# Two combines taken apart tile by tile, and a down projection moved ahead of the last expert tile

## What is computed

```python
def rmsnorm(x, g):
    y = xf * lax.rsqrt(jnp.mean(xf * xf, axis=-1, keepdims=True) + EPS)
    return (y * g).astype(x.dtype)

for l in range(DEPTH):
    u = modulate(rmsnorm(h, norm_mix[l]), m_lat[0], m_lat[1])
    ...
    h = h + m_lat[2] * y
    v = modulate(rmsnorm(h, norm_ffn[l]), m_lat[3], m_lat[4])
    f = hier_moe(v)
    h = h + m_lat[5] * f
return rmsnorm(h, norm_final)
```

## Time and profile before

| | |
|---|---|
| median of three runs | 2790.07 us (2789.45 to 2794.46) |
| the profiled execution's own time | 2781.04 us |
| its span, first to last instruction | 2779.2 us |
| PE busy | 2543.3 us, 92% of the span |
| DVE, ACT, POOL busy | 1035.4, 330.2, 238.7 us |
| combine to first projection, layer 0 | 1586.4 to 1632.4 us |
| first addition of the last combine to the end of the span | 2741.25 to 2779.2 us |

### The profile page before, as it was taken

How to read it: one execution, slowest core, us unless ns; L and a number is a source line. 1 busy time by engine, 2 the same in 40 slices (tenths; PEclk the granted TensorE clock), 3 DMA queues, 4 the chain that set the end, 5 groups by cost and what they waited for, 6 DMA issues and landing times. The chain is left out here.

```text
span 2779.2 us, 32467 instructions
## 1 busy us (share of the span) xinstructions
PE 2543.3 (92%) x14177; PEld 1115.0 (40%) x14178; DVE 1035.4 (37%) x1986; ACT 330.2 (12%) x640; POOL 238.7 (9%) x225
## 2 busy tenths in 40 slices
PE   6999999989999979999999769999997999999991
PEld 2556455544445533333333334444454333333330
DVE  2855246774845632222222241101364222222214
ACT  3100123331101100000000030000011000000001
POOL 2000000002830000000000000000000000000000
PEclk8888988998999979999999779999996999999996
DMA  9663000021030179999999531101004899999975
GB/s 331 211 241 136 16 23 23 23 99 61 0 113 39 65 296 388 390 378 398 386 376 386 202 107 46 46 23 61 16 31 187 332 386 373 385 396 390 368 307 230
DMA packets 121866, 574.11 MB, mean 207 GB/s; under 512 B 11743, under 2 KB 48807, under 8 KB 94712
## 3 DMA queue, kind: packets, MB, share of 16 engines
q1 hardware_dynamic: 103016, 523.32, 49.3%
q0 software_dynamic: 18704, 48.66, 4.5%
HBM read 550.71 MB, written 38.01 MB: 212 GB/s over the span
## 5 line engine op out<-in xcount | busy, mean ns | idle before, releaser
L1536 PE MATMUL ps<-arena 128*32 128x512 f32 x6144 | 695.6, 606 | 43.5 <-DMA arena<-in_ex_w_dram 43.5
L1536 PEld LDWEIGHTS ps<-arena 128*32 128x32 f32 x6144 | 199.8, 111 | 471.2 <-issue 471.2
L1560 PE MATMUL ps<-arena 128*32 128x512 f32 x3072 | 342.9, 598 | 22.7 <-DMA arena<-in_ex_w_dram 22.6
L1636 PE MATMUL ps<-arena 128*128 128x512 f32 x768 | 331.7, 595 | 1.8 <-ACT arena L833 1.8
L2156 DVE TENSOR_SCALAR arena<-ps,gain_x,mod 128x128 f32<-128x128 f32 x384 | 126.8, 403 | 380.0 <-PE ps L1521 380.0
L1413 PE MATMUL ps<-arena 128*128 128x512 f32 x512 | 228.5, 601 | 7.6 <-DVE arena L2264 6.1
L1636 PEld LDWEIGHTS ps<-arena 128*128 128x128 f32 x768 | 146.6, 191 | 186.5 <-issue 186.5
L1560 PEld LDWEIGHTS ps<-arena 128*32 128x32 f32 x3072 | 107.9, 111 | 248.7 <-issue 248.6
L2188 DVE SCALAR_TENSOR_TENSOR arena<-ps,arena,gates 128x512 f32<-128x512 f32 x96 | 72.1, 751 | 267.8 <-PE ps L1560 267.8
L1230 PE MATMUL ps<-arena 128*128 128x512 f32 x384 | 167.3, 593 | 0.7 <-ACT arena L863 0.7
L2164 DVE TENSOR_TENSOR arena<-arena,ps 128x512 f32<-128x512 f32 x48 | 52.6, 1096 | 275.0 <-PE ps L1536 275.0
(11 more groups left out here) (266 smaller groups left out, 2159.9 us busy)
## 6 DMA issues: line engine op xcount, KB each, us to landing
arena<-in_ex_w_dram SPq DMA_DIRECT2D x192, 2048.0 KB, 13.1
arena<-in_mod_w_dram SPq DMA_DIRECT2D x24, 2048.0 KB, 9.5
arena<-expert_rows SPq DMA_DIRECT2D x16, 1024.0 KB, 8.1
arena<-in_od_w_in_dram SPq DMA_DIRECT2D x24, 512.0 KB, 6.6
normed_rows<-arena POOLq DMA_DIRECT2D x16, 512.0 KB, 2.9
arena<-in_ev_w_in_dram SPq DMA_DIRECT2D x3, 2048.0 KB, 13.7
arena<-in_ev_w_in_dram SPq DMA_DIRECT2D x12, 512.0 KB, 4.1
arena<-in_x_dram POOLq DMA_DIRECT2D x1, 4096.0 KB, 22.0
```

The costliest lines, as they stand in the source:

```text
L1536: ins = nc.tensor.matmul(bank(2 + m)[c:c + n], x[:, j, c:c + n], w_slot(e % 2, m, KC, FE)[:, j], start=j == 0, stop=j == KC - 1)
L1560: ins = nc.tensor.matmul(bank(5 + half)[c:c + n], HT[:, j * P + c:j * P + c + n], w_slot(e % 2, 2, FC, D)[:, j, half * 512:(half + 1) * 51 ...
L1636: ins = nc.tensor.matmul(bank(2 * k + half), w[:, k, j], u_part(half, j), start=j == 0, stop=j == KC - 1)
```

## The change

It has four parts.

1. *Last pass.* On PE the down projection of pass 22 stands ahead of the up projections of pass 23 instead of behind them; on DVE the scaling of pass 22 stands ahead of the hidden product of pass 23. SP's loads are not changed.
2. *Pair sums.* For tiles 1, 3, 5 and 7 of each combine POOL adds the two expert rows (`pair_sums`), and DVE adds that sum to `H`: one addition of DVE instead of two, and one more of POOL.
3. *Norm by tile.* After layer 0 each tile goes through square, root, norm, transposition and columns as soon as it is combined. The norm moves from DVE (line 1686) to ACT (`row_of`). The copies of the gate rows stand after tile 3's addition. PE starts the first column block with the first half of the tokens, when tiles 0 to 3 have their columns, and does the second half afterwards. After layer 1 the mean square, the root and the final product of tile i - 1 stand between the additions of tiles i and i + 1, and the wait for `norm_final` stands ahead of the first addition.
4. *Small ones.* The constants count on the semaphore of the conditioning vector; the filter's hidden rows are stored from ACT's queue instead of POOL's.

POOL:

```diff
+            def pair_sums(l):
+
+                for i in range(1, TT, 2):
+                    pool.wait_ge(cy_full[i % NCY], 16 * (l * TT // NCY + i // NCY + 1))
+                    nc.gpsimd.tensor_tensor(CY[:, i % NCY, 1], CY[:, i % NCY, 0], CY[:, i % NCY, 1], ALU.add)\
+                        .then_inc(pair_sum, 1)
+                    pool.wait_ge(pair_sum, l * (TT // 2) + i // 2 + 1)
```

ACT, for every tile (the loop is that after layer 0):

```diff
+            def squares_and_root(n, i):
+                act.wait_ge(cy_used, TT * (n // 2 - 1) + i + 1)
+                if i >= 2:
+                    act.wait_ge(sq_done, norm_base[n] + i - 1)
+                nc.scalar.activation(at(32768, 2, D)[:, i % 2], H[:, i], ACT.Square, accum_out=ss[:, i:i + 1])\
+                    .then_inc(sq_done, 1)
+                act.wait_ge(ms_ready, root_base[n] + i + 1)
+                nc.scalar.activation(rstd[:, i:i + 1], rstd[:, i:i + 1], ACT.Sqrt).then_inc(root_ready, 1)
...
+                def row_of(i):
+                    act.wait_ge(rstd_ready, i + 1)
+                    if i >= 2:
+                        act.wait_ge(xn_T, norm_base[2] + i - 1)
+                    nc.scalar.activation(XN2[:, i % 2].rearrange("t (c p) -> t p c", p=P),
+                                         H[:, i].rearrange("t (p c) -> t p c", c=KC), ACT.Copy,
+                                         scale=rstd[:, i:i + 1]).then_inc(xn_ready, 1)
...
+                for i in range(TT + 1):
+                    if i < TT:
+                        squares_and_root(2, i)
+                    if i:
+                        columns_of(i - 1)
+                    if i < TT:
+                        row_of(i)
```

PE, the last passes and the start of the short convolution:

```diff
                 for p in range(NP):
+                    if p == NP - 1:
+                        pass_down(p - 1)
                     pass_ups(p)
-                    if p:
+                    if 0 < p < NP - 1:
                         pass_down(p - 1)
...
+                for i in range(5):
+                    turn_rows(i)
+                pe.wait_ge(u_ready, norm_base[2] + 4)
+                pe.wait_ge(u_act, norm_base[2] + 4)
                 pe.wait_ge(mod_gate, 8)
+                slab_in(L1_IN, 3)
+                for k in range(3):
+                    od_part(0, k, 0)
+                    if k + 5 < TT:
+                        turn_rows(k + 5)
                 pe.wait_ge(u_ready, norm_base[2] + TT)
                 pe.wait_ge(u_act, norm_base[2] + TT)
-                for c in range(KC):
+                for k in range(3):
+                    od_part(0, k, 1)
```

DVE, the additions and the two loops around them:

```diff
+            def add_rows(l, i, between):
+
+                if i % 2:
+                    between()
+                    dve.wait_ge(pair_sum, l * (TT // 2) + i // 2 + 1)
+                else:
                     dve.wait_ge(cy_full[i % NCY], 16 * (l * TT // NCY + i // NCY + 1))
                     link(V.tensor_tensor(H[:, i], H[:, i], CY[:, i % NCY, 0], ALU.add))
-                    V.tensor_tensor(H[:, i], H[:, i], CY[:, i % NCY, 1], ALU.add).then_inc(cy_used, 1)
+                    between()
+                V.tensor_tensor(H[:, i], H[:, i], CY[:, i % NCY, 1], ALU.add).then_inc(cy_used, 1)
...
+                for i in range(TT + 2):
+                    if i < TT:
+                        add_rows(0, i, (lambda: mean_square(2, i - 1)) if i else (lambda: None))
+                    elif i == TT:
+                        mean_square(2, i - 1)
+                    if 0 < i <= TT:
+                        inverse_root(i - 1)
+                    if i == 3:
+                        gate_rows(1)
+                    if i >= 2:
+                        columns_of(i - 2)
...
+            def combine_and_finish():
+
+                dve.wait_ge(small_in, SMALL0 + 64 * (DEPTH - 1) + 16)
+                for i in range(TT + 1):
+                    if i < TT:
+                        add_rows(1, i, (lambda: mean_square(4, i - 1)) if i else (lambda: None))
+                    else:
+                        mean_square(4, i - 1)
+                    if i:
+                        dve.wait_ge(root_ready, root_base[4] + i)
+                        link(V.reciprocal(rstd[:, i - 1:i], rstd[:, i - 1:i]))
+                        V.scalar_tensor_tensor(out=H[:, i - 1], in0=H[:, i - 1], scalar=rstd[:, i - 1:i], in1=GF,
+                                               op0=ALU.mult, op1=ALU.mult).then_inc(o_ready, 1)
```

More of the change, by code:

```diff
@@ L1054, in _ @@
                 if l:
-                    norm(2, H, at(32768, 2, D))
-                    columns(2, lambda i, j: U[:, j, i * P:(i + 1) * P])
+                    normed_rows_and_columns()
                     od_gates()
@@ L1061, in _ @@
                 overflow(l)
-            norm(4, H, at(32768, 2, D))
+            for i in range(TT):
+                squares_and_root(4, i)
         @block.tensor
@@ L1619, in shortconv, with turn_rows @@
                 gate_rows(1)
[L1620 to L1622 removed]
+                def turn_rows(i):
+                    pe.wait_ge(xn_ready, norm_base[2] + i + 1)
+                    if i >= 2:
+                        pe.wait_ge(u_ready, norm_base[2] + i - 1)
+                        pe.wait_ge(u_act, norm_base[2] + i - 1)
+                    for j in range(KC):
+                        ins = nc.tensor.transpose(bank(TURN_BANKS[i % 2][j // 4])[:, (j % 4) * P:(j % 4 + 1) * P],
+                                                  XN2[:, i % 2, j * P:(j + 1) * P], ident)
+                    ins.then_inc(xn_T, 1)
@@ new lines, in od_part @@
+                def od_part(c, k, half):
+                    for j in range(KC):
+                        ins = nc.tensor.matmul(bank(2 * k + half), slab(L1_IN + c, 3, KC, P)[:, k, j], u_part(half, j),
+                                               start=j == 0, stop=j == KC - 1)
+                    ins.then_inc(od_mm, 1)
+                for i in range(5):
+                    turn_rows(i)
+                pe.wait_ge(u_ready, norm_base[2] + 4)
+                pe.wait_ge(u_act, norm_base[2] + 4)
@@ L2236, in overflow @@
                 dve.sem_inc(ov_left, 1)
-            def final():
-                dve.wait_ge(sq_done, norm_base[5])
-                V.tensor_scalar(rstd[:, 0:TT], ss[:, 0:TT], 1.0 / D, EPS, ALU.mult, ALU.add).then_inc(ms_ready, 1)
-                dve.wait_ge(root_ready, root_base[5])
-                link(V.reciprocal(rstd[:, 0:TT], rstd[:, 0:TT]))
-                dve.wait_ge(small_in, SMALL0 + 64 * (DEPTH - 1) + 16)
-                for i in range(TT):
-                    V.scalar_tensor_tensor(out=H[:, i], in0=H[:, i], scalar=rstd[:, i:i + 1], in1=GF,
-                                           op0=ALU.mult, op1=ALU.mult).then_inc(o_ready, 1)
@@ L2274, in _ @@
                 overflow(l)
-                combine(l)
-            final()
+                if l == 0:
+                    combine_and_turn()
+                else:
+                    combine_and_finish()
 _INS = ['x', 'c', 'ctx', 'c_ctx', 'mod_w', 'mod_b', 'norm_mix', 'norm_ffn', 'norm_final', 'ev_w_in', 'ev_w_out',
```

90 lines of the change are left out of this document (54 added, 36 removed).

## The result

The changed kernel took 2798.78 us (median of 20 runs, 2779.78 to 2804.25), the kernel before on the same chip 2790.45 us (median of 20, 2780.57 to 2804.19). The ratio is 1.0029 with a 95% interval of 1.0017 to 1.0040: slower, by 0.3% or about 8 us. The forecast was 2798.9.

A forecast was written before the change was run, and what follows sets the result against it. PE, busy 92% of the span, was taken as the bound, with time to win only where it stands still. Last passes +5.4, middle -8.2, end +11.6 gave +8.8 on 2790.1: 2798.9 us, range 2785 to 2808.

The forecast's parts named there:

- The stall is moved: Last pass, both layers: the wait moves to expert 30's down weight and a hand-over is exposed; +5.4 us together.
- A: Layer 0, from the first rows scaled of pass 21 to the last rows scaled: +2.0 us forecast.
- C: Layer 1, from the first rows scaled of pass 21 to the last rows scaled: +3.4 us forecast.
- The price of a POOL sum: Combines: each pair sum holds DVE's additions 2.1 us and saves one of 1.23, so 0.9 us is lost.
- My two bounds for the end: Program end: +4.5 us if POOL hides completely, +15 us with 3.2 us for each sum.
- The rival in which POOL adds at no cost: Both combines: POOL adds beside DVE without holding it; in all -0.8 us, 2789; chance 0.20.
- B: After layer 0, from the first addition to the end of the first column block: -8.2 us forecast.
- My walk: After layer 0, engines' new orders followed with row durations: DVE's beat 4.6 us a tile, first column block done about 1647.0.
- D: Last rows scaled to the span's end: +11.6 us from the `norm_final` wait, POOL sums, and stores waiting for all additions.
- what I said the profile would show: Signs, among them: eight stores issued within 4 us, first column block some 60 us after the first addition instead of 68.8.
- The sum: Whole kernel: +5.4 - 8.2 + 11.6 = +8.8 us, added to the median of 2790.1.

The follow-up runs named there:

- the experiment without sums: Changed kernel with both additions of every tile on DVE, no POOL pair sums: 2792.34 us (1 run); end stretch 55.7 us against 59.0.
- Norm in order: Changed kernel with ACT's norm written in the order it is read, column permutation left out: 2777.31 us (1 run); middle stretch 78.5 us against 80.9.
- The two experiments on the end: Changed kernel with the `norm_final` wait behind the second tile's additions, then also without the stores' wait for all additions: end stretch 55.9, then 49.8 us, against 59.0.
- the last kernel: Changed kernel with pass 22's down projection between pass 23's up projections, no pair sums, later `norm_final` wait, stores by tile: ratio 0.9934 to the kernel before.
- the run with stores by tile: Changed kernel with the `norm_final` wait behind the second tile's additions and SP's stores not waiting for all additions: 2768.53 us (1 run).

## Why the prediction was right

**The stall is moved (A and C).** Right in place and cause, and in size as far as it can be told. Layer 0: +2.0 forecast and measured. Layer 1: +3.4 against +2.7. That layer 0 agrees to a tenth is luck: PE reached the end of its wait 0.4 us later than I had it, and the down projection behind it took 8.90 us and not 9.33. The size itself varies: over the seven kernels with this order A is 45.7 to 46.9 and C 44.6 to 49.2 us, over the two with the old order and an unmoved down projection 43.6 to 43.7 and 43.5 to 44.8.

**The price of a POOL sum.** I took 2.1 us. The four DVE additions beside a sum took 3.30, 2.49, 3.31 and 3.30 us, so they were held 2.1, 1.3, 2.1 and 2.1, in all 7.5 against 8.4. Three sums hold DVE for almost all of POOL's 2.34 us; the second had run for 0.9 us when DVE came to it. Saving four additions of 1.23, DVE loses 2.6 us on this; the experiment without sums won 3.4, nearly all of the difference being the longer wait for ACT's first square sum. My two bounds for the end don't follow from my own terms: 33.3 less 8.4 leads to 2770.3 and +3.2, not to 2771.5 and +4.5, and 3.2 us for each sum to +16, not +15. The rival in which POOL adds at no cost falls.

What no row had shown is in the profile after, at tile 4 of the middle:

```profile
1627.51 3.25 POOL L792 TENSOR_TENSOR arena<-arena 128x1024 f32<-128x1024 f32 x1 [6.35 <-DMA arena<-expert_rows]
```

```profile
1627.33 1.22 DVE L2317 TENSOR_TENSOR arena<-arena 128x1024 f32<-128x1024 f32 x1
...
1628.54 1.35 DVE L2328 TENSOR_SCALAR arena<-ps,gain_x,mod 128x128 f32<-128x128 f32 x4
```

DVE's columns, whose input comes from PSUM (`ps`), ran beside POOL's sum in 1.35 us, as long as before. And when DVE's addition came first, it took its 1.22 us and POOL's sum was held instead, 3.25 us and not 2.34.

**The middle (B).** -8.2 forecast, -8.5 measured, but two terms in it were wrong. That they did no harm is luck. First, one product of half the tokens is 16 instructions on PE (7.03 us, L1680), not eight. My walk counted eight and put the end of the first column block 68.8 us after the first addition before and 60.6 after; it was 89.4 and 80.9. The error was the same on both sides. What counts is when PE starts and what is put between the products: it starts 33.6 us after the first addition (32.2 forecast) instead of 46.0, which gains 12.4, and the block takes 47.3 us instead of 43.4 (three turns of 0.9 and a wait of 1.7, together 4.5, less 0.6 that its products took less than before), which gives 3.9 back. Second, ACT's norm takes 2.05 and not 1.15 us. The beat is therefore 5.5 us and not 4.6, but the 2.5 us of the gate rows, which I had added to DVE's path, hide behind ACT, but for some 0.2 us at tile 3 (1625.36 to 1631.05, 5.7 us): tile 4 is turned 31.8 us after the first addition, and my walk had 31.1. The longer beat and the hidden copies offset each other. "Norm in order" shows the other side of this: with 1.15 us DVE is the pacer and the gate rows come back as the beat of 6.6.

**The end (D).** +11.6 forecast, +10.2 measured. The wait for `norm_final` puts the first addition 4.2 us later after the last rows scaled, as forecast (15.1 instead of 10.9). DVE up to the last addition's end 31.8 us against 33.3; 0.9 of the difference is POOL's second sum. The small operations (0.15 where I had up to 0.2) and the products were shorter too, by 1.8 us in all, but 1.2 of that went into a wait for ACT's first square sum, which my sum didn't have. Stores and what follows: 12.1 as forecast. Of what I said the profile would show, one thing was wrong beside the two times of the column block: the eight store issues took 7.9 us and not under 4; the DMA was full at 404 GB/s, and the end came at the same time. The two experiments on the end split D's loss of 10.2: 3.1 us for the wait (of its 4.2, since the first pair sum then sets the start), 6.1 for the stores, and the rest, 0.9 over the end before, is less than the 3.4 of the pair sums, so the end by tiles seems to have a gain of its own, some 2.4 us, that the sums eat; the last kernel, whose D is 1.8 below the one before, points the same way.

**The sum.** +8.8 forecast, +6.4 by the profiles' four stretches, +8.3 by the medians. The difference between the last two is within what the untouched stretches vary; that they vary with PE's clock is shown by the two windows above, but not that this is all of it. So the causes were right, but the median of 2798.8 beside a forecast of 2798.9 is luck: by the stretches the sum was 2.4 us too high, 1.4 of it in D and 0.7 in C, and the stretches without a forecast gave the rest.

## What to carry to other kernels

Before an instruction that waits for a load is moved forward, ask when its own load is issued and how long that takes: the down weight of pass 22 can be issued only when pass 21's down projection has run, and lands some ten us later. The remedy for two loads in a row was to put the work between them, not ahead of them. Giving POOL every fourth addition of a DVE that is the bottleneck lost time, because a sum of POOL and a two-input operation of DVE exclude each other; it cost nothing, and won nothing, where ACT set the pace. And taking an end apart tile by tile bought nothing while its last link, the stores, still waited for all; whether it pays with the stores taken apart too (1.6 us of D, 0.7 between the medians) is open.

## What the runs showed of the hardware

ACT's copy of 128x1024 values took 2.05 us when each value was written 128 values behind the one before, and 1.15 us when written in order, though it read in order both times. DVE's final product, which reads two inputs from the same memory, was held by a POOL sum just as an addition is: in the run with stores by tile one took 3.37 us instead of 1.28. One product of half the tokens is eight matmuls in the program and 16 instructions in the trace (7.03 us at full clock).

```profile
2751.95 3.37 DVE L2360 SCALAR_TENSOR_TENSOR arena<-arena,rstd 128x1024 f32<-128x1024 f32 x1
```
